# Second attention of the second block: score products of the two heads of a pair follow each other by size, and the gate's running sums stand in rows 0 and 64 as 384 columns

## The reference, cut to what matters

```python
f_logit = jnp.einsum('bsd,dh->bhs', h, w_fg[j]) + b_fg[j][None, :, None]
log_f = jax.nn.log_sigmoid(f_logit.astype(jnp.float32))
o = forgetting_attention(q, k, v, log_f)

def forgetting_attention(q, k, v, log_f):
    cum = lax.cumsum(log_f, axis=2)
    for blk in range(s_len // Q_BLOCK):          # Q_BLOCK = 128: two blocks
        z = jnp.einsum('bhqd,bhkd->bhqk', qb, kb) * scale
        decay = cum[:, :, q0:k_end, None] - cum[:, :, None, :k_end]
        logits = jnp.where(s_idx <= t_idx, z + decay, -jnp.inf)
        p = jax.nn.softmax(logits, axis=-1)
        outs.append(jnp.einsum('bhqk,bhkd->bhqd', p, vb))
```

## Time and profile before

| | before |
|---|---|
| median of 3 launches | 1655.16 us (1644.07 to 1662.22) |
| the profiled launch | 1651.79 us |
| its span, first to last instruction | 1650.1 us |
| mean granted TensorE clock | 0.981 of full |
| busy: PE, PEld | 1517.0 us (92%), 997.3 us (60%) |
| busy: DVE, ACT, POOL | 385.8 us, 317.2 us, 19.5 us |

### The profile page before, as it was taken

One profiled execution on the slowest core, in us unless ns is written; L12 is line 12 of the kernel. 1 busy time (PEld: TensorE's weight loads), 2 busy tenths in 40 slices (PEclk: granted clock), 3 DMA queues, 4 the chain that ended last, 5 costly groups with the idle time before them and its releaser, 6 DMA issues.

```text
span 1650.1 us, 20867 instructions
## 1 busy us (share of the span) xinstructions
PE 1517.0 (92%) x7992; PEld 997.3 (60%) x7993; DVE 385.8 (23%) x750; ACT 317.2 (19%) x550; POOL 19.5 (1%) x63
## 2 busy tenths in 40 slices
PE   5999999888888888887999999999989999999998
PEld 2776885644545544444584557777768444677775
DVE  1346554400000000000301422111121043211112
ACT  1220001311222221212302531111130133211111
POOL 2000000000000000000000000000000000000000
PEclk8999999999999999999999999999999989999999
DMA  9655414689999999999844961444284374244420
GB/s 375 231 198 229 180 47 180 246 333 412 426 426 426 426 427 427 426 425 424 308 153 157 353 221 38 152 152 152 77 303 153 142 261 159 102 153 153 153 76 26
DMA packets 87372, 400.51 MB, mean 243 GB/s; under 512 B 5489, under 2 KB 10737, under 8 KB 61713
## 3 DMA queue, kind: packets, MB, share of 16 engines
q1 hardware_dynamic: 87312, 399.66, 61.7%
HBM read 398.60 MB, written 1.05 MB: 242 GB/s over the span
## 4 chain that ended last, share of the span: by engine, by line
PE 76%; DMA 11%; issue 4%; DVE 4%; ACTq 2%; ACT 2%; SPq 0%; DVEq 0%; PEldq 0%
PE psum L1256 19%; PE psum L950 9%; PE psum L1269 9%; PE psum L1079 7%; DMA ring<-in_moe_gate 6%; DMA ring<-in_moe_up 4%; PE psum L564 3%; PE psum L1219 3%; PE psum L1100 3%; PE psum L501 3%; DMA ring<-in_ada_w 1%; PE psum L696 1%; PE psum L714 1%; PE psum L708 1%; PE psum L900 1%
## 5 line engine op out<-in xcount | busy, mean ns | idle before, releaser
L950 PE MATMUL psum<-ring,arena 128*64 128x512 f32 (+1 forms) x2496 | 344.7, 428 | 36.1 <-issue 18.8
L1256 PE MATMUL psum<-arena,ring 128*128 128x256 f32 x1408 | 312.2, 380 | 0.1
L1256 PEld LDWEIGHTS psum<-arena,ring 128*128 128x128 f32 x1408 | 268.1, 191 | 54.1 <-issue 19.5
L950 PEld LDWEIGHTS psum<-ring,arena 128*64 128x64 f32 x2496 | 193.9, 137 | 170.1 <-issue 95.9
L1269 PE MATMUL psum<-ring,arena 128*128 128x512 f32 x352 | 157.9, 592 | 0.0
L1079 PE MATMUL psum<-arena,ring 128*128 128x256 f32 x512 | 113.3, 384 | 0.2
L1079 PEld LDWEIGHTS psum<-arena,ring 128*128 128x128 f32 x512 | 98.5, 193 | 15.0 <-issue 1.4
L1269 PEld LDWEIGHTS psum<-ring,arena 128*128 128x128 f32 x352 | 66.9, 190 | 66.3 <-issue 63.1
L1903 DVE TENSOR_SCALAR arena<-psum,cols 128x256 f32<-128x256 f32 x44 | 23.9, 544 | 327.8 <-PE psum L1256 327.8
L2239 ACT ACTIVATE arena<-arena 128x256 f32<-128x256 f32 x44 | 18.3, 416 | 394.6 <-DVE arena L1909 394.6
L1702 DVE TENSOR_TENSOR arena<-psum,arena 128x256 f32<-128x256 f32 x32 | 13.6, 425 | 312.3 <-ACT arena L2099 304.1
(11 more groups left out here) (379 smaller groups left out, 1283.8 us busy)
## 6 DMA issues: line engine op xcount, KB each, us to landing
ring<-in_moe_down SPq DMA_DIRECT2D x32, 2048.0 KB, 19.9
ring<-in_moe_up SPq DMA_DIRECT2D x31, 2048.0 KB, 18.5
ring<-in_moe_gate SPq DMA_DIRECT2D x31, 2048.0 KB, 19.9
ring<-in_w_mod SPq DMA_DIRECT2D x24, 2048.0 KB, 7.5
ring<-in_ada_w SPq DMA_DIRECT2D x12, 2048.0 KB, 10.4
ring<-in_w_qkv SPq DMA_DIRECT2D x12, 2048.0 KB, 15.2
ring<-in_w_ffn_gate SPq DMA_DIRECT2D x10, 2048.0 KB, 7.8
ring<-in_w_ffn_up SPq DMA_DIRECT2D x10, 2048.0 KB, 12.6
```

The lines of the kernel that those rows point to most:

```text
L950: ins = mm(bank[b][o, 0:n], lhsT, w[:, half * n:(half + 1) * n], start=first, stop=last, tile_position=(0, 64 * half))
L1256: last = mm(b[:, k * TOK:(k + 1) * TOK], sl[k][2][:, c, j * P:(j + 1) * P], hTd[:, c, :], start=(c == 0), stop=(c == DC - 1))
```

## The change: what it does

In layer 1 `scores(m)` first issues the two products of 128 columns over 64 rows, one for each head, then the two of 256 columns, then for each head one gate product of 384 columns, where there were two. For the second head the gate product now reads rows 64 to 79. So the gate's sums have to stand in rows 0 to 15 and in rows 64 to 79, and as 384 columns: the first 128 tokens, then all 256. They lie in a new tile `cum3`. To get them into both places, `wfg` is widened to 80 columns, with the weights in columns 0 to 15 and 64 to 79 and zeros between, the bias stands in `fg_bias` twice, and all steps of the gate run on 80 partitions. The negated copy is dropped; in its place 128 columns are copied inside `cum3`. In layer 0 the code of `scores` is written in another form and issues the same products in the same order.

```diff
+NH2 = 80
...
-        wfg = at(20480, DC, NHA)
+        wfg = at(21120, DC, NH2)
+        cum3 = at(21760, 384)
+        fg_bias = at(22144, 2)
...
-                    sp.wait_ge(S("x2_ready"), 2)
-                    sp.dma_start(wfg, a["w_fg"].rearrange("(c p) n -> p c n", p=P)).then_inc(S("fg_in"), 16)
+                    sp.wait_ge(S("neg_made"), 1)
+                    for o in (0, 64):
+                        sp.dma_start(wfg[:, :, o:o + NHA], a["w_fg"].rearrange("(c p) n -> p c n", p=P)).then_inc(S("fg_in"), 16)
+                        sp.dma_start(fg_bias[o:o + NHA, :], a["cols"][0:NHA, COLS["b_fg"][0] - 1:COLS["b_fg"][0] + 1])\
+                            .then_inc(S("fg_in"), 16)
...
             pool.wait_ge(S("x2_ready"), 2)
+            g(nc.gpsimd.memset(wfg, 0.0))
+            g(nc.gpsimd.memset(fg_bias, 0.0))
...
-                            last = mm(bank[7][0:NHA, 0:TOK], wfg[:, c, :], hTd[:, c, :], start=(c == 0),
+                            last = mm(bank[7][0:NH2, 0:TOK], wfg[:, c, :], hTd[:, c, :], start=(c == 0),
...
+                    else:
+                        for z, hs in zip(zs, rows_of):
                             mm(z[:, 0:128], QT[hs, m, 0:P], KT[hs, m, 0:P], start=True, stop=False, skip_group_check=True)
+                        for z, hs in zip(zs, rows_of):
                             mm(z[:, 128:384], QT[hs, m, P:TOK], KT[hs, m, :], start=False, stop=False,
                                skip_group_check=True)
-                            one = ident[0:NHA, h:h + 1]
-                            last = mm(z[:, 0:128], one.broadcast_to([NHA, P]), ncumf[0:NHA, 0:P], start=False,
-                                      stop=False, skip_group_check=True)
-                            last = mm(z[:, 128:384], one.broadcast_to([NHA, P]), ncumf[0:NHA, :], start=False,
+                        for hh, z in enumerate(zs):
+                            hs, h = slice(64 * hh, 64 * hh + NHA), 64 * hh + 2 * m + hh
+                            last = mm(z[:, 0:384], ident[hs, h:h + 1].broadcast_to([NHA, P]), cum3[hs, :], start=False,
                                       stop=True, skip_group_check=True)
...
-                    H_ = slice(0, NHA)
+                    H_ = slice(0, NH2)
...
-                    d(V.tensor_tensor_scan(out=u_, data0=keep1, data1=v_, initial=0.0, op0=ALU.mult, op1=ALU.add))
-                    d.to(V.tensor_scalar(v_, u_, -1.0, None, ALU.mult), "cum_ready")
+                    d(V.tensor_tensor_scan(out=cum3[H_, P:384], data0=keep1, data1=v_, initial=0.0, op0=ALU.mult, op1=ALU.add))
+                    d.to(V.tensor_copy(cum3[H_, 0:P], cum3[H_, P:2 * P]), "cum_ready")
```

More of the change, by code:

```diff
@@ L138, in build_program @@
         level = sb("level", [P, 6, P])
-        keep1 = level[0:NHA, 1:3, :].rearrange("p a b -> p (a b)")
+        keep1 = level[0:NH2, 1:3, :].rearrange("p a b -> p (a b)")
         modc = sb("modc", [P, 3, 48])
@@ L1083, in _ @@
                     if layer == 1 and q == 0:
-                        pe.wait_ge(S("fg_in"), 16)
+                        pe.wait_ge(S("fg_in"), 64)
                         for c in range(DC):
-                            last = mm(bank[7][0:NHA, 0:TOK], wfg[:, c, :], hTd[:, c, :], start=(c == 0),
+                            last = mm(bank[7][0:NH2, 0:TOK], wfg[:, c, :], hTd[:, c, :], start=(c == 0),
                                       stop=(c == DC - 1))
@@ L1114, in scores @@
                     if m >= 3:
[L1115 to L1123, removed]
+                        pe.wait_ge(S("prob_ready" if layer == 0 else "pt_copied"), m - 2)
+                    zs = [bank[1 + 2 * (m % 3) + hh] for hh in range(2)]
+                    rows_of = [slice(64 * hh, 64 * hh + 64) for hh in range(2)]
+                    if layer == 0:
+                        for z, hs in zip(zs, rows_of):
                             mm(z[:, 0:256], KT[hs, m, 0:P], QT[hs, m, :], start=True, stop=False, skip_group_check=True)
@@ L1127, in scores @@
                                       skip_group_check=True)
-                        else:
+                    else:
+                        for z, hs in zip(zs, rows_of):
                             mm(z[:, 0:128], QT[hs, m, 0:P], KT[hs, m, 0:P], start=True, stop=False, skip_group_check=True)
+                        for z, hs in zip(zs, rows_of):
                             mm(z[:, 128:384], QT[hs, m, P:TOK], KT[hs, m, :], start=False, stop=False,
                                skip_group_check=True)
-                            one = ident[0:NHA, h:h + 1]
-                            last = mm(z[:, 0:128], one.broadcast_to([NHA, P]), ncumf[0:NHA, 0:P], start=False,
-                                      stop=False, skip_group_check=True)
-                            last = mm(z[:, 128:384], one.broadcast_to([NHA, P]), ncumf[0:NHA, :], start=False,
+                        for hh, z in enumerate(zs):
+                            hs, h = slice(64 * hh, 64 * hh + NHA), 64 * hh + 2 * m + hh
+                            last = mm(z[:, 0:384], ident[hs, h:h + 1].broadcast_to([NHA, P]), cum3[hs, :], start=False,
                                       stop=True, skip_group_check=True)
@@ L1780, in _ @@
                     dve.wait_ge(S("fg_done"), 1)
-                    H_ = slice(0, NHA)
+                    H_ = slice(0, NH2)
                     u_, v_ = ncumf[H_, :], cumf[H_, :]
-                    d(V.tensor_scalar(u_, bank[7][H_, 0:TOK], col("b_fg")[H_, :], -1.0, ALU.add, ALU.mult))
+                    d(V.tensor_scalar(u_, bank[7][H_, 0:TOK], fg_bias[H_, 1:2], -1.0, ALU.add, ALU.mult))
                     d(V.tensor_scalar(v_, u_, 0.0, None, ALU.max))
```

## The result

The changed kernel takes 1628.7 us (median of four, 1627.23 to 1630.93), the kernel before, with a fourth launch on the same chip, 1652.39 us. The ratio is 0.9862, with a 95% interval of 0.9828 to 0.9896: faster by 1.4%.

The account below looks back on a forecast made before the run. Taken as bound by TensorE in the second attention, layer 1 scores about a quarter of it, partly at half clock. Scores 13.4 − lateness 0.4 + clock 8.2 = 21.2 us off 1655.2 gives 1634.0 us; range 1626 to 1646.

Parts of the forecast that it names:

- The score products: Layer 1 scores on TensorE: both heads overlap, a pair takes 1.71 us for 3.39, eight pairs save 13.4 us.
- 0.21 us around each run: Layer 1 score runs: time beyond the columns, where TensorE goes from 64 rows to 16 and back; four runs become two.
- Slower, if each step from row 0 to row 64 cost as much as one from 64 rows to 16: Rival, score products: each of six carries 0.21 us, 3.82 us a pair, clock 5.3 us more; 1663.9 us; chance 0.03.
- The clock: Second attention: of 19.5 us at half clock, one 3.2 us stretch stays and the rest returns, giving 8.2 us.
- the first rival: Second attention: the clock stays low as before; only 13.0 us come, 1642.2, or 1639.4 if low for a third; chance 0.16.
- a second stretch, around the flush: Second attention: if transposes don't count as busy, a second fall of the clock stays, and the sum is 1.6 us less.
- What becomes late next: Loop of the second attention: DVE's mask in iteration 6 starts late, costing 0.4 us; ACT and tiles cost nothing.
- the same 13.7: End of the second attention: the 13.7 us of latency from the last scores to `w_o` doesn't shrink.
- Sum: Whole kernel: 13.4 − 0.4 + 8.2 = 21.2 us; the stage of 61.1 us becomes 39.9, the median 1634.0 us.
- Range: Whole kernel: 1626 to 1646 us, to hold 0.8, from full clock return (1632.4) to 1642.2, widened by a few us.
- At nothing: Preparation (SP's four transfers, POOL's fills, wider gate weight load, DVE's gate steps): expected to cost nothing.
- Something else sets the pace: Rival, loop of the second attention: DVE or the tiles hold it, leaving some 5 us of gain, 1650; chance 0.03.

Follow-up runs that it names:

- gate_row0: Changed kernel with both heads' gate products reading rows 0 to 15; 1635.0 us (four launches), ratio 0.9899 to the kernel before.
- gate_64rows: Changed kernel with the gate products over 64 rows (0 to 63 and 64 to 127) instead of 16, zeros added; 1629.22 us (six launches).
- old_gate128: Kernel with the change's preparation but the old scores in old order, gate products over all 128 rows; 1643.54 us, ratio 0.9944 to the kernel before.
- rest_only: Changed kernel with all its preparation kept but the scores of the kernel before; 1650.05 us (ten launches), ratio 1.0002 to the kernel before.
- heads_unsorted: Changed kernel with the 64-row products ordered 128, 256 of the first head, then 128, 256 of the second, then both gate products; 1634.65 us (one launch).
- by_head_64: Changed kernel with all three products of the first head, then all three of the second, gate products over 64 rows; 1633.91 us (one launch).

## Why the prediction was right

- **The score products**: 1.71 us was forecast for the pair, 1.70 measured; both gate products overlap, which no row of before had shown. That they would cost 1.49 us if they didn't is what gate_row0 measured. That the order by size adds nothing was right too. The "0.21 us around each run" was put down to the change of the row size. gate_64rows takes one such change out and gets 0.20 us a pair, and old_gate128 shows 0.09 us of it, at the end of a product, only where the number of rows changes.
- **Slower, if each step from row 0 to row 64 cost as much as one from 64 rows to 16**: didn't occur; such steps cost nothing, those of the row size do.
- **The clock**: 8.2 us were forecast to come back, the half of 19.5 less 1.6 for one stretch that stays. The stretches in the earlier trace rows leave out their edges: the clock records have 20.5 us at 0.50. Up to the last scores all of it came back, about 9.8 us (old_gate128 has 9.2 of it, and 0.5 of waits against that). One stretch stayed, as forecast, but in the last part of the stage, where TensorE waits for some of the time, so it cost 0.95 us and not 1.6: the last transposes take 1.33 us for 0.71 before, and the four wide passes behind them 2.14 for 1.81 (lines below). The clock gave 8.8 us, then, 0.6 more than the forecast. old_gate128 shows the cause apart from the overlap: rows at work. So the first rival (the clock stays) was wrong. The Trainium skill ("TensorE: Matmul & The Clock Gate", PE-mode transpose) says that transposes don't count as busy for the clock the way other products do. By that rule a second stretch, around the flush, was to stay. None fell there in the loop; the one that fell came after transposes, flush and waits, and one such case settles nothing. The end of the stage in the changed kernel, and before:

```profile
1348.70 1.54 PE L1159 MATMUL psum<-ident,arena 128*128 128x128 f32 x6 [0.57 <-DVE arena L1849]
1350.03 2.21 PE L838 MATMUL psum<-arena,ones 128*128 128x512 f32 x4
1352.17 0.66 PE L1175 MATMUL psum<-arena 128*64 128x256 f32 x4
...
1374.04 0.87 PE L1158 MATMUL psum<-ident,arena 128*128 128x128 f32 x6 [0.93 <-DVE arena L1848]
1374.75 1.88 PE L830 MATMUL psum<-arena,ones 128*128 128x512 f32 x4
1376.56 0.66 PE L1174 MATMUL psum<-arena 128*64 128x256 f32 x4
```

- **What becomes late next**: 0.4 us was too little. That the mask of pair 7 is late was right, and it costs the 0.4 us forecast: the transposes of pair 6 begin 4.30 us after the last scores for 3.91 before. Not in the forecast was what VectorE holds up in the loop: TensorE stands 0.3 us for it at pair 0 (the first iterations are 3.5 us long, under VectorE's 4.1) and 0.35 at the flush of iteration 4. From the last scores to `w_o` it is 15.05 us for 13.72, where "the same 13.7" was forecast; the 1.3 us are the 0.4 of the mask and the 0.95 of the clock.
- **Sum**: 13.4 + 8.8 − 1.1 = 21.1 us, and 21.0 measured in the stage, for 21.2 forecast. The mechanism was right in both its large terms; that the sum came out to 0.2 us is luck, since 0.6 us too little for the clock and 0.7 too little for VectorE cancel. The medians differ by 23.7 us; the attention happened to begin 3.4 us earlier in the changed kernel's profile, and the two sets of launches scatter by more than that.
- **Range**: 1628.7 lies in it, but 5.3 us from the forecast and near the lower end: the prediction's working for that end, 1632.4 less the 3.8 us of the other end, makes 1628.6, and 1626 is wider than that. In the first rival, 38.1 us should be 38.3 (61.1 − 9.8 − 13.4 + 0.4), which moves its 1639.4 by 0.2.
- **At nothing**: rest_only bears it out at 1.0002. One item was off, but had room: the four issues on SP, thought to take some 2 us. SP needed from 809.33 to 819.17 us for the four transfers, and the next tile went out at 824.02 when its slot came free:

```profile
809.33 0.58 SPq L351 DMA_DIRECT2D arena<-in_w_fg  x1
809.95 5.50 SPq L352 DMA_DIRECT2D arena<-in_cols  x1
815.50 0.48 SPq L351 DMA_DIRECT2D arena<-in_w_fg  x1
816.02 3.15 SPq L352 DMA_DIRECT2D arena<-in_cols  x1
824.02 0.37 SPq L275 DMA_DIRECT2D ring<-in_w_mod  x1
```

- **Something else sets the pace**: the tiles didn't, at 353 GB/s over the loop. VectorE is the next: its scaled probabilities are what TensorE waits for longest in the stage, 1.3 us before, 1.6 now and 2.4 in gate_64rows.

## What to carry to other kernels

Before reordering small products, look in the trace for one place where two of them in different rows start within some tens of ns, and price the pair from there. What kept them apart here was mostly a product of another row count between them, and padding the product of 16 rows to 64 with zeros took no more time on TensorE and removed the gap. Where TensorE is busy but its clock falls, count the rows at work: here products over 64 and 16 rows, one at a time, left the engine 100% busy with the clock at half for 20.5 of 57.6 us, and that was worth nearly as much as the overlap. When a loop on TensorE gets shorter, write down the work of the next engine per iteration, in the first iterations and the last as well, before trusting the sum.

## What the runs showed of the hardware that was not expected

- Widening products from 16 rows to 128, with zeros, made the program faster by 0.56% (0.9944, 0.9927 to 0.9962). In the stage 9.2 of the 9.8 us are the clock and 0.6 one change of the row size less per pair; the columns and the time of a product stayed the same (0.49 us for 0.48, 0.60 for 0.59).
- A transfer of 16 rows of 8 bytes held SP for 5.50 and 3.15 us when issued right behind one of 1024 pieces of 64 bytes, which itself took SP 0.5 us. In the nine other profiles with these transfers it was 4.0 to 5.5 us and 3.1 to 3.3. Whatever stood behind it on that queue waited as long. Whether it waits for the transfer ahead of it or is itself so slow to issue wasn't tried.
- Passes of different row groups don't start in the order of the program. In heads_unsorted the second head's product of 128 columns stands behind all four passes of the first head, and starts at 1324.013 us, ahead of the first head's product of 256 columns (1324.325) and 0.013 us after the first head's own of 128. With six passes ahead (by_head_64) it starts 0.34 us after it.
